# A two-layer hybrid transformer on one core: the mixers' output projection by blocks of tokens, and feed-forward stages linked by waits

## The reference

```python
for l in range(DEPTH):
    with_ctx = l < DEPTH - 1
    hl = modulate(rms_norm(xl, g[0]), mod_l[0], mod_l[1])
    mc, ml = hybrid_mixer(hc, hl, ...)          # its last step: concatenate four groups, @ w_out (1024 x 1024)
    xl = xl + mod_l[2] * rms_norm(ml, g[1])
    hl = modulate(rms_norm(xl, g[2]), mod_l[3], mod_l[4])
    xl = xl + mod_l[5] * rms_norm(swiglu(hl, ffn_w_in[l], ffn_w_out[l]), g[3])
    # the same for xc, with its own modulation, where with_ctx
def swiglu(h, w_in, w_out):                      # w_in 1024 x 5632, w_out 2816 x 1024
    gate, up = jnp.split(h @ w_in, 2, axis=-1)
    return (jax.nn.silu(gate) * up) @ w_out
def rms_norm(x, g):
    return x * rsqrt(mean(x * x) + 1e-6) * g
```

## Time and profile before

| | us |
|---|---|
| median of 3 runs | 4217.67 |
| lowest and highest of them | 4212.2, 4218.17 |
| the profiled execution | 4221.19 |
| its span in the trace | 4219.4 |
| TensorE busy in it | 3569.6 (85%) |
| layer 0, mixers' projection (TensorE's first to last product) | 112.8, from 1105.55 |
| layer 0, from there to the first product of the feed-forward | 47.87 |
| layer 0, second feed-forward product of the third block (256 tokens) | 115.26, from 2197.79 |

### The profile page before, as it was taken

How to read it: one execution, slowest core, us unless ns; L and a number is a source line. 1 busy time by engine, 2 the same in 40 slices (tenths; PEclk the granted TensorE clock), 3 DMA queues, 4 the chain that set the end, 5 groups by cost and what they waited for, 6 DMA issues and landing times. The chain is left out here.

```text
span 4219.4 us, 56278 instructions
## 1 busy us (share of the span) xinstructions
PE 3569.6 (85%) x20754; PEld 2940.9 (70%) x20754; DVE 1755.9 (42%) x2494; ACT 1594.7 (38%) x2693; POOL 541.4 (13%) x929
## 2 busy tenths in 40 slices
PE   4998786896769999999886899767986779999997
PEld 3997454774558877877786799544774658787876
DVE  3112655776334522532452211555776345323322
ACT  3011455775233422422442211445775234223222
POOL 0001363121001100100100000444221011000000
PEclk8999886998889999999998899978998889999999
DMA  4224411004214323323443123612003133233323
GB/s 172 90 69 146 161 57 44 8 7 164 95 61 139 104 84 110 114 80 101 152 137 107 65 90 107 221 53 61 8 5 132 40 109 115 81 97 130 95 82 107
DMA packets 145410, 401.03 MB, mean 95 GB/s; under 512 B 15696, under 2 KB 79888, under 8 KB 138384
## 3 DMA queue, kind: packets, MB, share of 16 engines
q1 hardware_dynamic: 112848, 328.45, 24.2%
q0 software_dynamic: 11712, 43.00, 2.8%
q10 hardware_dynamic: 20736, 28.18, 1.9%
HBM read 337.32 MB, written 57.02 MB: 93 GB/s over the span
## 5 line engine op out<-in xcount | busy, mean ns | idle before, releaser
L759 PE MATMUL psum<-part,part 128*128 128x512 f32 (+2 forms) x4240 | 1526.8, 360 | 225.0 <-DVE part L1690 218.5
L760 PE MATMUL psum<-part,part 128*128 128x512 f32 (+2 forms) x4240 | 1515.9, 358 | 0.0
L761 PE MATMUL psum<-part,part 128*128 128x512 f32 (+2 forms) x4240 | 1514.7, 357 | 0.0
L759 PEld LDWEIGHTS psum<-part,part 128*128 128x128 f32 x4240 | 815.2, 192 | 335.4 <-issue 223.1
L1690 DVE TENSOR_TENSOR part<-region,part 128x1024 fp32r<-128x1024 f32 (+5 forms) x446 | 562.7, 1263 | 1111.7 <-ACT part L1572 546.2
L760 PEld LDWEIGHTS psum<-part,part 128*128 128x128 f32 x4240 | 815.3, 192 | 94.7 <-issue 1.0
L761 PEld LDWEIGHTS psum<-part,part 128*128 128x128 f32 x4240 | 814.1, 192 | 94.7
L1572 ACT CAST part<-region 128x1024 fp32r<-128x1024 f32 x220 | 230.5, 1048 | 488.9 <-PE psum L761 434.3
L2023 DVE TENSOR_REDUCE region<-psum 128x1 f32<-128x1280 f32 (+1 forms) x216 | 295.1, 1369 | 168.0 <-PE psum L1012 168.0
L1545 ACT CAST part<-region 128x1408 fp32r<-128x1408 f32 (+1 forms) x96 | 126.7, 1319 | 464.2 <-DMA region<-in_ffn_out 360.7
L1455 ACT ACTIVATE region<-psum,region 128x1280 f32<-128x1280 f32 (+1 forms) x216 | 266.7, 1235 | 92.2 <-DVE region L2023 91.9
(11 more groups left out here) (221 smaller groups left out, 3257.0 us busy)
## 6 DMA issues: line engine op xcount, KB each, us to landing
region<-in_ffn_in SPq DMA_DIRECT2D x220, 512.0 KB, 3.6
region<-in_ffn_out SPq DMA_DIRECT2D x80, 704.0 KB, 4.0
region<-in_ada_w SPq DMA_DIRECT2D x14, 2048.0 KB, 9.7
proj<-region ACTq DMA_DIRECT2D x16, 1720.0 KB, 11.3
region<-proj SPq DMA_DIRECT2D x20, 1376.0 KB, 8.8
region<-in_w_in SPq DMA_DIRECT2D x16, 1376.0 KB, 7.2
region<-in_ada_w SPq DMA_DIRECT2D x20, 1024.0 KB, 6.3
region<-proj SPq DMA_DIRECT2D x116, 128.0 KB, 2.3
```

Of the source, the lines that this page charges most:

```text
L759: mm(out, a[0], b[0], start=start, stop=False)
L760: mm(out, a[0], b[1], start=False, stop=False)
L761: return mm(out, a[1], b[0], start=False, stop=stop)
```

## The change

The mixers' projection becomes `mix_out`. Its steps go block by block: 8 chunks of features for the first block of tokens, then the 8 for the second, then for the third. Weights are loaded and split in the first block's steps only. All 8 chunks stay in the arena (`WO`) and serve the other blocks. Each step uses one of two PSUM banks (`y_bank`).

The first block's norm is no longer a stage. It is a `Weave` over the second block's steps (`mix_weave`), with GpSimd adding up the squares. The sums for the roots of y are made block by block. Those of the later blocks are rooted in `hidden`.

Between `hidden` and `project_back` there is no handover any more, nor between `project_back` and the next block's `hidden`. TensorE waits for `act_ready`, SP waits for `gate_made`, `wb_ready` or `yb_made`, and the first split of the next stage is issued before the last steps of the stage that ends. The third block's hidden values are packed closer, and its two units get a `raw` place each.

The diff, without the repeated parts:

```diff
+            def __init__(self, r, first, per, lag=1):
-                self.x_summed = first + units + 3
+                self.x_summed = first + units + 2 + lag
                 self.scale = {k: self.x_summed + 1 + k // per for k in range(KD)}
-                self.round = {k: u + 1 for k, u in self.scale.items()}
-                self.rest = {k: u + 2 for k, u in self.scale.items()}
+                self.round = {k: u + lag for k, u in self.scale.items()}
+                self.rest = {k: u + lag + 1 for k, u in self.scale.items()}
...
+        def back(l, block):
+            nb, j = len(blocks(l)), block[0] - blocks(l)[0][0]
+            return KH // 2, W_AT, *before(l, KD, nb + 2 * j, nb + j, 2 * j), block[1], block[2]
+        def before(l, first, made, kept, loaded):
+            nb = sum(len(blocks(m)) for m in range(l))
+            return KD * (l + 2 * nb + loaded) + first, KD * (3 * nb + made), KD * (2 * nb + kept)
+        WO = [[Y1 + 2 * N + (2 * c + i) * KD * P for i in range(2)] for c in range(KD)]
+        def mix_weave(l):
+            return Weave(renewals(l, False)[0], 0, 4, 0)
+        def unit_slots(block):
+            second = W_AT if block[2] == FFN_T else ACT_HI + KH * block[2]
+            return [W_AT, second], [W_AT + i * UNIT for i in (1, 3)], [W_AT + i * UNIT for i in (2, 4)]
...
+            def mix_out(l):
+                units = before(l, 0, 0, 0, 0)[0]
+                for c in range(KD):
+                    sp.wait_ge(sem("wb_ready"), units + c + 1)
+                    sp.dma_start(region(WO[c][1], KD * P), t["w_out"][l, c]).then_inc(sem(f"wb_in{c % 2}"), 16)
+                handover("sp", sp)
...
+                sp.wait_ge(sem("gate_made"), (block[0] + 1) * KH + 1)
+                with sp.Fori(0, KD) as u:
+                    for j in range(2):
+                        sp.wait_ge(sem("wb_ready"), units + 2 * u + j + 1 + single)
+                        sp.dma_start(region(raw[j], kk * P), t["ffn_out"][l, u, :, j * kk * P:(j + 1) * kk * P]
+                                     ).then_inc(sem(f"wb_in{j}"), 16)
+                if not after(l, block):
+                    handover("sp", sp)
...
-                with sp.Fori(0, KH) as u:
+                _, _, units, made, _, _, _ = back(l, block)
+                sp.wait_ge(sem("wb_ready"), units + 2)
+                for u in range(2):
                     for half in range(2):
+                        if u == 0 and half == 1:
+                            sp.wait_ge(sem("yb_made"), made + 1)
                         sp.wait_ge(sem(f"wf_ready{half}"), block[0] * KH + u + 1)
                         sp.dma_start(region(WF[half][0], KD * P), t["ffn_in"][l, u, half]
                                      ).then_inc(sem(f"wf_in{half}"), 16)
-                handover("sp", sp)
...
+                total = region(squares_at(r.is_ffn)[0], N)
+                mm(r.y_root(), ones[:], total[:, r.a:r.b], start=True, stop=True).then_inc(sem("y_summed"), 1)
+            def sum_added(r):
+                pe.wait_ge(sem("sq_total"), sum_totals(r) + 1)
+                pe.wait_ge(sem("h_normed"), r.given * KD)
+                mm(r.x_root(), ones[:], r.y(0), start=True, stop=True).then_inc(sem("x_summed"), 1)
...
-            def project_back(l, block=None):
-                per, kk, src_at, _, w_at, units, chunks, t0, n = back(l, block)
-                src = [region_r(at, KD if per == 1 else KH, N if per == 1 else FFN_T) for at in src_at]
-                pieces = spans(t0) if per == 1 else [(0, n)]
-                first = t0 if per == 1 else 0
-                _, hi, lo = unit_slots(w_at, block, kk * P)
+            def mix_out(l):
+                units, _, kept = before(l, 0, 0, 0, 0)
+                src = [region_r(at, KD, N) for at in (MIX_HI, MIX_LO)]
+                rs, weave = renewals(l, False), mix_weave(l)
+                for i, ((_, t0, n), c) in enumerate(mix_steps(l)):
+                    if i < KD:
+                        pe.wait_ge(sem("wb_ready"), units + c + 3)
+                    pe.wait_ge(sem("yb_kept"), kept + i + 1)
+                    w = [region_r(at, KD, P) for at in WO[c]]
+                    for k in range(KD):
+                        last = mm3(y_bank(c % 2)[:, 0:n], [x[:, k, :] for x in w], [x[:, k, t0:t0 + n] for x in src],
+                                   start=(k == 0), stop=(k == KD - 1))
+                    last.then_inc(sem("yb_made"), 1)
+                    if i >= KD and c == 0:
+                        pe.wait_ge(sem("sq_added"), kept + i + 1)
+                        sum_y(rs[i // KD - 1])
+                    if i - KD == weave.x_summed:
+                        sum_added(rs[0])
+                pe.wait_ge(sem("sq_added"), kept + i + 2)
+                sum_y(rs[-1])
+                handover("pe", pe)
+            def project_back(l, block):
+                kk, _, units, _, kept, t0, n = back(l, block)
+                src = [region_r(at, KH, n) for at in (ACT_HI, ACT_LO)]
+                _, hi, lo = unit_slots(block)
...
+                        for j in range(2):
+                            w = [region_r(at, kk, P) for at in (hi[j], lo[j])]
+                            pe.wait_ge(sem("wb_ready"), units + 2 * (2 * u + s) + j + 3)
+                            pe.wait_ge(sem("act_ready"), block[0] * KH + (j + 1) * kk)
                             if j == 0:
+                                pe.wait_ge(sem("yb_kept"), kept + 2 * u + s + 1)
+                            for k in range(kk):
+                                last = mm3(y_bank(s)[:, 0:n], [x[:, k, :] for x in w], [x[:, j * kk + k, :] for x in src],
+                                           start=(j == 0 and k == 0), stop=(j == 1 and k == kk - 1))
                             last.then_inc(sem("yb_made"), 1)
-                handover("pe", pe)
+                if not after(l, block):
+                    handover("pe", pe)
...
                     if r.is_ffn:
+                        units(done, w_.y_rooted)
+                        done = w_.y_rooted
+                        pe.wait_ge(sem("sq_added"), back(l, block)[4] + 1)
                         sum_y(r)
+                        sum_added(r)
                 units(done, KH)
-                handover("pe", pe)
...
+            def unit_hi(l, block, c, j):
+                kk, _, units, made, _, _, _ = back(l, block)
+                raw, hi, _ = unit_slots(block)
+                m = 2 * c + j
+                act.wait_ge(sem(f"wb_in{j}"), 8 * (units + m - j) + 16)
+                act.wait_ge(sem("yb_made"), made + m + 1)
+                nc.scalar.copy(region_r(hi[j], kk * P), region(raw[j], kk * P)).then_inc(sem("wb_hi"), 1)
+            def half_hi(l, block, u, half):
+                index = block[0]
+                if u == FIRST:
+                    act.wait_ge(sem("yb_made"), back(l, block)[3] + 1 + half)
+                act.wait_ge(sem(f"wf_in{half}"), 16 * (index * KH + u + 1))
+                act.wait_ge(sem("up_made" if half else "gate_made"), index * KH + u + 1)
+                nc.scalar.copy(region_r(WF[half][1], KD * P), region(WF[half][0], KD * P)
+                               ).then_inc(sem(f"wf_hi{half}"), 1)
...
+                act.wait_ge(sem("sq_added"), kept + 1)
+                act.wait_ge(sem("yb_made"), made + 2)
+                activation(region(squares_at(is_ffn)[1], N)[:, t0:t0 + n], y_bank(s)[:, 0:n], ACT.Square
+                           ).then_inc(sem("sq_made"), 1)
+                nc.scalar.copy(dst_at, y_bank(s)[:, 0:n]).then_inc(sem("yb_kept"), 1)
+            def mix_out(l):
+                units, made, kept = before(l, 0, 0, 0, 0)
+                steps, weave = mix_steps(l), mix_weave(l)
+                def keep(i):
+                    (_, t0, n), c = steps[i]
+                    keep_y(kept + i, made + i + 1, region(H_HI, KD, N)[:, c, t0:t0 + n], False, c % 2, t0, n)
+                for i, (_, c) in enumerate(steps):
+                    if i < KD:
+                        act.wait_ge(sem(f"wb_in{c % 2}"), 8 * (units + c - c % 2) + 16)
+                        nc.scalar.copy(region_r(WO[c][0], KD * P), region(WO[c][1], KD * P)).then_inc(sem("wb_hi"), 1)
+                    if i:
+                        keep(i - 1)
+                    renew_at(weave, i - KD)
+                keep(len(steps) - 1)
+                handover("act", act)
...
+                following = after(l, block)
+                if following:
+                    half_hi(l, following, FIRST, 0)
                 keep(KD - 1, 1)
-                handover("act", act)
+                if not following:
+                    handover("act", act)
...
+                if block == blocks(l)[0]:
+                    half_hi(l, block, FIRST, 0)
+                half_hi(l, block, FIRST, 1)
...
+                units, _, kept = before(l, 0, 0, 0, 0)
+                steps, weave = mix_steps(l), mix_weave(l)
+                def add(i):
```

(34 more changed lines are left out.)

243 lines of the change are left out of this document (103 added, 140 removed).

## The result

The changed kernel takes 4040.56 us (median of 4 runs, 4036.45 to 4043.43). The kernel before, run beside it, takes 4216.40 us (4 runs, 4212.20 to 4218.17). The ratio is 0.9584, with a 95% interval of 0.9567 to 0.9600. The prediction was 4052 us with a range of 4026 to 4090. Seven further kernels and the changed kernel once more were run after that. One of them, which sums the squares on two engines, takes 4018.94 us and beats both.

What follows compares the result with a forecast made beforehand. TensorE's idle time and half-clock time were taken as the bound. Terms of 73.5 - 30.7 + 46.1 + 27.4 + 49.3 = 165.6 us off 4221.19 gave 4055.6, stated as 4052 us for the median, range 4026 to 4090.

Steps and rivals of the forecast that it cites:

- Term 1: Between mixers' projection and hidden stage, the norm's stage goes: 73.5 us gained, a border of 9.4 us left.
- Term 2: Weaving in the mixers' projection costs TensorE 30.7 us, with a 9.9 us wait a layer for the sum of squares.
- Terms 3 and 4: Earlier loads shorten the borders: hidden stage to second product, 46.1 us; second product to next hidden stage, 27.4 us.
- E: End of the hidden stage; the second product's first split was put at E + 1.9 us, with 256 tokens E + 4.4.
- Term 5: Third block's second product in layer 0: two raw places cut 115.26 us to 66 us, 49.3 us gained.
- The rival that the sum is in time: Mixers' projection: TensorE does not wait for the sum of squares, giving 25 us, 4027 us; chance 0.08.
- The rival that GpSimd's rounds grow: Mixers' projection: VectorE and GpSimd block each other, 3 us a layer, 4058 us; chance 0.08.
- The loads do not bound the third block: Answers the rival that loads keep the third block at 5.6 us a unit, 24 us lost, 4076 us; chance 0.12.
- the borders closed: Answers the rival that some 5 us and the low clock stay at eight linked borders, 36 us, 4088; chance 0.12.
- the slower case: Mixers' projection: keep, add and split do not fit, each 512-token step waits 3.6 us, 4340 us; chance 0.02.

Runs made afterwards that it cites:

- both late-load experiments: Changed kernel with one load issued one wait later: a second product's first unit, 4071.40 us; the next block's first unit, 4064.14 us.
- the repeat: The changed kernel run once more, unchanged, as yardstick for three later kernels: 4040.08 us.
- two experiments: Changed kernel with one raw place again in the third block: 4087.97 us; kernel before with only packed values and two raw places there: 4167.82 us.

## Why the prediction was right, point by point

- **Term 1 (73.5 us), the norm's stage.** Right. The left-over border was put at 9.4 us and is 8.22 and 8.67: 1.9 us more gained in the two layers together.
- **Term 2 (-30.7 us), the weaving.** The mechanism was right in place, releaser and order: one wait, at the fifth step, behind GpSimd's last addition. Its size was off: 9.9 us a layer was forecast, 7.11 and 8.57 measured, because the chain used the whole root of 3.9 us and rounds of 3.0 us. A round that nothing holds up is 2.87 us; in layer 1 the longer rounds took that back. The clock behind it was put at 2.6 us a layer. Layer 0's window loses 2.7 (10 us at 0.73), layer 1's 1.6 (at 0.84); removing the wait gave back some 3.4 and 1.0. The two terms together forecast 42.8 us, and 50.7 came. The wait, the border and the clock make 7 us of that difference, nearly all of the error of the sum (172.9 against 165.6).
- **Terms 3 and 4 (46.1 and 27.4 us), the links.** 73.3 us came where 73.5 were forecast. The seams are 1.98, 2.0, 2.0, 1.9 and 4.25 us, as worked out (1.9 and 4.4), and both late-load experiments brought the gaps back with their clock. The working has a slip here: 5.42 us before E, plus 4.0, 1.36 and 1.62, is E + 1.6 and not E + 1.9, and with 256 tokens E + 4.1. The waits between the steps, which it left out, take the other 0.2 to 0.4 us. And the closeness of the sum is in part luck, for two errors cancel. The clock behind a 2 us seam fell to 0.83 behind two of the four, 1.7 us each, which takes what the last row but one of the table lacks (8.7 against 10.4). In layer 0's third hidden stage TensorE waited 3.5 us less than before. The prediction reads that it never waits inside the other feed-forward stages; in this one it waited 16.1 us before, 12.6 now and 11.7 in the repeat, mostly for the split of weights.
- **Term 5 (49.3 us), two raw places.** 66.32 us against 66, shown from both sides by two experiments.
- **The rival that the sum is in time (4027 us)** fell, but it described the better kernel: the split sum took 4018.94 us, 21 us below the changed one.
- **The rival that GpSimd's rounds grow** was right in its cause, and its 3 us a layer came nearly whole in layer 1 only. The Trainium skill, page "SBUF — State Buffer", section "Who interferes with whom", says that such VectorE and GpSimd instructions exclude each other; the rows of both kernels agree (3.26 us became 5.98 with two additions of 1.30 inside, and 4.74 with one). But VectorE was the one that mostly waited, and it had time there. GpSimd was held up too: in layer 0 by 0.9 us (the first addition, 2.20 instead of 1.30), in layer 1 by 0.65 (1.95 instead of 1.30) and by 2.0 in the one long round, whose cause is not shown. That is 0.9 and 2.7 us of the waits of 7.11 and 8.57. Six rounds of 2.87 us and the 1.86 from the last addition's start to the product (1176.35 to 1178.21) are 19.1 us, so the forecast's 21.0 had 1.9 to spare: more than layer 0's loss, less than layer 1's.
- **The other rivals.** The loads do not bound the third block, the borders closed, and no step of the projection waits for keep, add or split, so the slower case had no ground. Its assumption that the clock stays at its lower level with a wait in every step was not tested; in the third block's second product before, where TensorE waited in nearly every unit, the mean clock was 0.85.
- **What the range rests on.** The unchanged part ahead of the projection moves by up to 11 us between executions. A forecast made from one profiled execution is uncertain by as much; the 8.6 us by which this part was shorter here are as large as the error of the terms.

## What to carry to other kernels

When one stage is woven into another, follow the single chain that crosses both, and count at which step TensorE meets its end; a serial sum on a slow engine (2.87 us a tile here) is the first suspect, and splitting it over two engines costs TensorE one product of 0.9 us instead of seven. A ring of load, cast and subtraction through one buffer bounds a stage as soon as a unit's products are shorter than the ring (3.95 against 7.2 us), and a second buffer alone removes that. Stage borders cost their gap and some 2 us of clock behind it, so bringing a gap of 7 us down to 2 is worth more than its 5 us.

## What the runs showed of the hardware that was not expected

- ScalarE's table load (1.28 us) does not wait with the activation that needs it: it ran at 1144.18, the activation's input came at 1149.33.
- GpSimd's addition and VectorE's two-input instructions run one after the other, and in a set of eight VectorE pays about the length of each addition of 1.30 us: 1.03, 1.36 (the mean of two) and 1.48 us were read. Beside VectorE's additions with one input in PSUM neither lost time.
- A seam of 2 us may lower the clock or not, and not by its place. In the seven profiled executions with four such seams each, the repeat's among them, the 10 us behind them ran at 0.83 behind 16 and at 1.00 behind 12. Two executions of the same kernel had it behind different seams, as this window of the repeat shows, where the first execution had 0.83 at the same place:

```profile
1846.28:1856.28 10.00, 10.00 (x44) 8.28 (x45) 2.78 (x3) 2.00 (x2) 0.00 (x0) 1.00 0.43 131
```

- One round of GpSimd in layer 1 took 4.83 us instead of 2.87, and 4.51 in the repeat. VectorE's add of squares beside it took 2.28 instead of 0.69 us, so both were held up. In layer 0 of the repeat VectorE's adds took 2.02 and 2.20 us, and there the rounds stayed at 2.87. What held GpSimd stays open.
